# A two-block network on one core: hidden activations of the feed-forwards kept as high/low pairs, and the second output product run from its last column to its first

## The reference, cut to what matters

```
def _swiglu(x, w_in, w_out):                 # x (256, 1024), w_in (1024, 5632), w_out (2816, 1024)
    g, u = jnp.split(x @ w_in, 2, axis=-1)
    return (jax.nn.silu(g) * u) @ w_out      # hidden (256, 2816)

h = _swiglu(_rms_norm(x, ffn1_pre_norm), ffn1_w_in, ffn1_w_out)
x = x + 0.5 * _rms_norm(h, ffn1_post_norm)
...                                          # token mixing
h = _swiglu(_rms_norm(x, ffn2_pre_norm), ffn2_w_in, ffn2_w_out)
x = x + 0.5 * _rms_norm(h, ffn2_post_norm)
```

## Time and profile before

| what | value |
|---|---|
| median of three executions | 890.93 us (889.25 to 890.97) |
| span of the profiled execution, first to last instruction | 887.0 us |
| TensorE matmul busy | 879.6 us, 99% of the span |
| TensorE weight loads busy | 752.3 us, 85% |
| VectorE, ScalarE busy | 625.0 us (70%), 489.4 us (55%) |
| granted TensorE clock, mean | 0.999 |

### The profile page before, as it was taken

One profiled execution on the slowest core, in us unless ns is written; L12 is line 12 of the kernel. 1 busy time (PEld: TensorE's weight loads), 2 busy tenths in 40 slices (PEclk: granted clock), 3 DMA queues, 4 the chain that ended last, 5 costly groups with the idle time before them and its releaser, 6 DMA issues.

```text
span 887.0 us, 11473 instructions
## 1 busy us (share of the span) xinstructions
PE 879.6 (99%) x4628; PEld 752.3 (85%) x4628; DVE 625.0 (70%) x808; ACT 489.4 (55%) x661; POOL 64.4 (7%) x89
## 2 busy tenths in 40 slices
PE   9999999999999999999999999999999999999997
PEld 7888888888888888888888888888999888888886
DVE  6887776467767656577577777446979857888872
ACT  6865564445444556446565555435887644555551
POOL 2000000003021110000000000000390000000000
PEclk9999999999999999999999999999999999999999
DMA  9955555455753444455655555546534456555521
GB/s 352 368 188 191 191 189 199 147 190 179 282 198 127 180 168 173 184 190 190 237 190 190 191 190 190 189 182 251 184 106 181 151 187 254 190 190 191 190 95 48
DMA packets 26948, 169.89 MB, mean 192 GB/s; under 512 B 3616, under 2 KB 3664, under 8 KB 7952
## 3 DMA queue, kind: packets, MB, share of 16 engines
q1 hardware_dynamic: 24368, 161.23, 50.3%
q0 software_dynamic: 2240, 7.66, 2.5%
q10 hardware_dynamic: 288, 0.27, 0.1%
HBM read 167.05 MB, written 1.05 MB: 190 GB/s over the span
## 4 chain that ended last, share of the span: by engine, by line
PE 97%; DVE 1%; ACT 1%; issue 0%; ACTq 0%
PE acc L1839 15%; PE acc L1642 15%; PE acc L1640 15%; PE acc L1641 15%; PE acc L2101 8%; PE acc L1841 7%; PE acc L2103 4%; PE acc L1655 2%; PE acc L1883 2%; PE acc L2053 2%; PE acc L2054 2%; PE acc L2052 2%; PE aux L2037 1%; PE aux L1764 1%; PE acc L1885 1%; PE aux L1641 1%
## 5 line engine op out<-in xcount | busy, mean ns | idle before, releaser
L996 DVE TENSOR_TENSOR w_lo<-raw,w_hi 128x2048 fp32r<-128x2048 f32 x147 | 336.8, 2300 | 89.9 <-ACT w_hi L522 89.5
L522 ACT ACTIVATE w_hi<-raw 128x2048 fp32r<-128x2048 f32 x145 | 275.7, 1911 | 62.6 <-DMA raw<-weights 62.4
L1839 PE MATMUL acc<-xT,w_hi 128*128 128x512 f32 x576 | 200.4, 394 | 0.0
L1841 PE MATMUL acc<-xT,w_lo 128*128 128x256 f32 x576 | 159.7, 277 | 0.0
L1839 PEld LDWEIGHTS acc<-xT,w_hi 128*128 128x128 f32 x576 | 108.0, 188 | 25.0
L1640 PE MATMUL acc<-w_hi,xT 128*128 128x512 f32 x312 | 124.0, 398 | 0.0
L1642 PE MATMUL acc<-w_hi,xT 128*128 128x512 f32 x312 | 121.8, 390 | 0.0
L1641 PE MATMUL acc<-w_lo,xT 128*128 128x512 f32 x312 | 121.5, 390 | 0.0
L2101 PE MATMUL acc<-xT,w_hi 128*128 128x512 f32 x320 | 111.3, 394 | 0.0
L1841 PEld LDWEIGHTS acc<-xT,w_lo 128*128 128x128 f32 x576 | 108.2, 188 | 0.0
L2103 PE MATMUL acc<-xT,w_lo 128*128 128x256 f32 x320 | 88.7, 277 | 0.0
(11 more groups left out here) (263 smaller groups left out, 1290.4 us busy)
## 6 DMA issues: line engine op xcount, KB each, us to landing
raw<-weights SPq DMA_DIRECT2D x147, 1024.0 KB, 4.8
gain_pre<-gains POOLq DMA_DIRECT2D x5, 512.0 KB, 5.0
raw<-weights SPq DMA_DIRECT2D x4, 512.0 KB, 7.5
gain_post<-gains POOLq DMA_DIRECT2D x3, 512.0 KB, 5.6
gate_w<-gate_w_in POOLq DMA_DIRECT2D x1, 1536.0 KB, 8.5
x_turned<-x_turned_in SPq DMA_DIRECT2D x4, 256.0 KB, 4.9
x<-x_in SPq DMA_DIRECT2D x2, 512.0 KB, 11.6
bias_raw<-bias_in POOLq DMA_DIRECT2D x16, 64.0 KB, 3.2
```

The lines of the kernel that those rows point to most:

```text
L522: a.activation(w_hi[:, g % RING], raw[:, g % RING], ACT.Copy).then_inc(hi_done, 1)
L996: v.tensor_tensor(w_lo[:, slot], raw[:, slot], w_hi[:, slot].bitcast(F32), ALU.subtract)\
L1839: m.matmul(dst, w_hi[:, slot, w], xT[:, k].rearrange("p a q -> p (a q)"), start=k == 0, stop=False)
L1841: i = m.matmul(dst[:, 0:S], w_lo[:, slot, w], xT[:, k, 0], start=False, stop=k == KD - 1)
```

## The change

The two tiles become one, `hT`, of 128 x 22 x 256 x 2: the high and the low part of a token lie side by side. `hT_hi` and `hT_lo` are now views of it, and their 128 tokens stand 8 bytes apart. So the weight loads of both output stages read with a step of 8 bytes; ScalarE writes the high part and VectorE reads it and writes the low part with that step. The size of the area is the same.

In the second output stage (`f2_out`) each matmul streams its 512 weight columns from the last to the first, and writes its 512 sums into the accumulator from the last to the first. Each sum lands where it did. The first output stage goes forward as before. Every engine has the same instructions in the same order as before (4346 rows on TensorE, 662 on VectorE, 511 on ScalarE); only their access patterns differ.

```
-        hT_hi = at("hT_hi", [P, FF // P, S], F32R, area)
-        hT_lo = at("hT_lo", [P, FF // P, S], F32R, area + 22528)
+        hT = at("hT", [P, FF // P, S, 2], F32R, area)
+        hT_hi, hT_lo = hT[:, :, :, 0], hT[:, :, :, 1]
...
-            def product(dst, hi, lo, k, t, slot, unit, first, last):
+            def product(dst, hi, lo, k, t, slot, unit, first, last, backward=False):
 
                 cols = slice(t * P, (t + 1) * P)
                 w = slice(unit * UNIT, (unit + 1) * UNIT)
-                m.matmul(dst, hi[:, k, cols], w_hi[:, slot, w], start=first, stop=False)
-                m.matmul(dst, hi[:, k, cols], w_lo[:, slot, w], start=False, stop=False)
-                return m.matmul(dst, lo[:, k, cols], w_hi[:, slot, w], start=False, stop=last)
+                high, low = w_hi[:, slot, w], w_lo[:, slot, w]
+                if backward:
+                    dst, high, low = dst[:, ::-1], high[:, ::-1], low[:, ::-1]
+                m.matmul(dst, hi[:, k, cols], high, start=first, stop=False)
+                m.matmul(dst, hi[:, k, cols], low, start=False, stop=False)
+                return m.matmul(dst, lo[:, k, cols], high, start=False, stop=last)
...
                     for half in range(2):
-                        i = product(target(t, half), hi, lo, k, t, g % RING, 2 * kk + half, k == 0, k == chunks - 1)
+                        i = product(target(t, half), hi, lo, k, t, g % RING, 2 * kk + half, k == 0, k == chunks - 1,
+                                    backward=st == "f2_out")
```

## The result

The changed kernel takes 893.69 us (892.73 to 894.90, four runs) against 890.09 us (889.07 to 890.97, four runs) for the kernel before: a ratio of 1.0043, 95% interval 1.0027 to 1.006. The change costs 0.43%, some 3.6 us. The forecast was no change, 890.9 us. The time lies inside the stated range of 887.5 to 948 us, just beyond the forecast's own 888.5 to 893.5, and it is slower by more than a measurement can confuse with nothing, for which the prediction gave 0.36.

A forecast was written before the change was run, and what follows sets the result against it. TensorE's matmul stream was taken as the bound; 887.0 us of span + 0 (stepped loads) + 0 (ScalarE and VectorE writes) + 0 (direction), plus 3.9 us from span to median, gave 890.9 us, range 887.5 to 948 us.

The forecast's parts named there:

- What bounds the kernel: Whole kernel: TensorE's matmul stream alone sets the time, busy 879.6 of 887.0 us; both output stages have no idle time.
- The stepped loads: Both output stages: 528 weight loads stepping by 8 bytes stay hidden behind 512-column matmuls; cost 0, bounds 0 to 79 us.
- The writes of ScalarE and VectorE: Input stage: stepped rows, 36 each of two lines plus four larger, fit spare time; cost 0, 31 us if cover were gone.
- The direction: Second output stage: 264 backward matmuls keep 0.2264 us each; cost 0, between 3.4 us gained and 54.4 us lost.
- rival 1: Second output stage: backward matmuls pass columns at half rate, 0.206 us each, 54.4 us more, 945.3 us in all; chance 0.22.
- rival 2: Second output stage: fixed price per backward matmul, at its start or accumulator hand-over, at most 22 us, 913 us; chance 0.07.
- Only the second a little longer: Sign for rival 2: distance between matmul starts slightly above 0.2264 us in the second output stage, unchanged in the first.
- rival 3: Both output stages: stepped weight loads become the bound, 528 x 0.150 = 79 us at the far end, 970 us; chance 0.05.
- a small price above 1.8 us: Part of the forecast's case: small slowdowns beyond the 1.8 us a measurement can tell from no change; chance 0.02.
- a possible gain: Second or both output stages: the 0.013 us per matmul beyond columns goes away, 3.4 to 6.9 us gained; chance 0.05.
- The 3.9 us that the sum adds to the span: Whole kernel: the runs' median lies 3.9 us above the profiled span, added to 887.0 us to give 890.9 us.

## Why the prediction was wrong

*What bounds the kernel*: right. The loss is in the distance between matmuls in the two stages, and nothing hid it.

*The stepped loads*: this is the step that failed. It argued that a load holds its matmul up for 0.11 us at most and may double, so it costs 0. The first half nearly held: loads 122 ns longer cost 9 ns per matmul, so 5 to 10 ns more by themselves are no explanation for 6.6. But the sum treated load and stream as two things that meet only where one waits for the other. They also meet in what each matmul has above its columns. That remainder was in the prediction, 0.013 us per matmul, and was set aside since "no row ties it to how the load reads". The runs tie it: with the stepped loads it goes from 0.0133 to 0.0200 us, and as far at unchanged load rows of 188 ns when only the loads' place is moved. The term was 528 x 0; it measured 528 x 6.6 ns = 3.5 us. The bounds of 0 to 79 us held it.

*The writes of ScalarE and VectorE*: right. ScalarE's rows grew by 16 ns, 36 x 0.016 = 0.6 us in all, and a run with the step but without the writes lost as much.

*The direction*: the forecast's 264 x 0 came out in the sum, but by luck. By itself a backward read costs 6.6 ns per matmul, 264 x 6.6 ns = 1.7 us; it added nothing only because the stepped loads had already cost as much.

*Backward at half rate* (rival 1): wrong for direction, nearly right in price for something else. 0.4325 us was priced from the float32 row; a stream with an 8-byte step takes 0.4533.

*A fixed price per backward matmul* (rival 2): this is what a backward read alone does, at 6.6 ns and not the 84 of its bound; the accumulator, which the rival named as one place for it, has no part by these rows, since writing backward is free (0.2268 us). In the changed kernel it can't be seen, because the loads already cost as much. "Only the second a little longer: rival 2" was therefore no safe test: two prices that cover each other give equal stages.

*Stepped loads as the bound* (rival 3): right in its sign, both stages longer alike, but not in its mechanism, since it begins only where a load's part before its matmul has more than doubled, and the loads' rows grew by 5 to 10 ns in 188.

*The chances*: the slower rivals were thought of as large, up to 22, 54 and 79 us; a small price above 1.8 us was given 0.02. A remainder of 0.013 us, worth 6.9 us over 528 matmuls, was counted as a possible gain and hardly as a thing that could grow. The 3.9 us that the sum adds to the span was a mixture too: a run of the changed kernel takes 1.7 us beyond its own span (892.73 and 891.0), and the other 2 us come from the spread of the three runs before.

What stays open: why the place counts. The matmul's row grows with the distance (397 ns in place of 389), so the streamed read or its start may be what is slowed; that, and that both reads collide in the memory, is argued, not shown. Open also is what puts the untouched input stage into one pace or the other.

## What to carry to other kernels

A hidden operation may be free in its duration alone: here what the critical engine spends per instruction beyond its own work depended on how the hidden one reads. So measure the distance between starts, take off the useful part, and treat the rest as a term with both signs. Before blaming an access pattern for a few ns per instruction, move the tile without the pattern: here a shift of 128 and 256 bytes cost what the pattern did, and one of 32 and 64 bytes two thirds of it. And test the parts of a change one at a time even where the profile seems to separate them, since prices may cover each other.

## What the runs showed of the hardware beside that

- The streamed operand is the sensitive one: every second float32 halves the rate (0.2267 to 0.4533 us), where a load with the same step takes 193 to 198 ns in place of 188 and stays hidden. A load with 16 bytes of step takes 310 ns, one of 64 columns 134.
- The Trainium skill ("SBUF — State Buffer", section "Specifications (TRN2)") asks for two hits or more per 16-byte line for full bandwidth, and has a penalty for each new line. With two hits per line the loads' rows are near to the full rate (193 to 198 ns in place of 188); the stream has half of it, so there two hits are not enough.
- Writing PSUM from the last column to the first costs nothing; reading from the last to the first costs 6.6 ns per matmul of 512 columns (0.2333 us), with plain loads.
- A stream that begins 4 bytes off the start of its 2048-byte unit costs 9.9 ns more per matmul (0.2367 us, one profile).
- The input stage, whose matmuls of 512 and 256 columns take turns, ran at 454 or at 463 matmuls in 80 us, both at a granted clock of 1.00; the slower pace also came without any change to the stage.
